# A two-layer decoder step on one core: order of the dense block's product and weight split, clearing of the query tables, the router's token rows, and where the expert gates are computed

## The chip, the cores and the metric

One NeuronCore of a Trainium2 chip runs one launch of a hand-ordered kernel: every engine (TensorE as PE, ScalarE as ACT, VectorE as DVE, GpSimd as POOL, SyncE as SP) has its own instruction list, and semaphores tie the lists together. The metric is the device time of the launch in microseconds (us), median of several runs.

## The reference, cut to what matters

288 tokens (256 of a prompt, 32 of eight sample requests) of width 1024 go through two layers, in float32.

```python
# each layer
x = x + rmsnorm_concat(mixer_a, mixer_b, mixer_x)(rmsnorm(x) @ w_in) @ w_out
# layer 0: dense SwiGLU, D_FF = 2816
x = x + (silu(h @ wg) * (h @ wu)) @ wd          # h = rmsnorm(x) * g_ffn[0]
# layer 1: 8 experts, D_FF_E = 3584, each token uses its 2 best
logits = h @ w_router                           # h = rmsnorm(x) * g_ffn[1]
vals, idx = top_k(logits, 2)
gates = one_hot(idx) weighted by softmax(vals)
x = x + sum_e gates[:, e] * swiglu(h, wg[e], wu[e], wd[e])
y = rmsnorm(x) * g_final
```

Further outputs are memory keys and values, pooling buffers and v rows of the mixers.

## The kernel before, in words

**Weight stream.** All weights come as 402 chunks of 128x2048 floats (1 MB). SP loads chunk c into one of six `raw` slots as soon as chunk c-6 is split (`load_chunk`, line 299). ACT copies it to `whi` as fp32r (line 306) once chunk c-3 has been used by PE, and DVE writes the remainder into `wlo` (line 310). Products use three matmuls each, hi x hi, hi x lo, lo x hi (`mm3`, lines 322 to 324). PE counts used chunks in `chunk_used`. `hi_static` and `lo_static` put these splits at fixed places in the lists of ACT and DVE, so the order of everything is written out by hand.

**Start.** PE turns the memory rows, computes keys and values of both layers (lines 1430 to 1450), turns x, spreads the row norms over all partitions (`spread_rstd`, line 1410; DVE scales the identity into `diag`, line 879, and keeps the product as `rB`, line 886), and begins layer 0.

**A layer's first part.** `queries(k)` for eight blocks, then four transposes of the keys (line 1476), which DVE copies as `kT` (line 925); DVE scales the queries into `qT` (line 921) and spreads the sample queries into the tables `qs_hi` and `qs_lo` (lines 937, 940), which POOL clears first (`zero_pair`, line 439). Scores are line 1490. In layer 1 POOL adds up the squares of x (`power_of_x`), PE sums them (`sums_of_x`, after `queries(5)`), DVE makes the mean, POOL the power -0.5, DVE `diag`, PE spreads it; POOL clears the two tables and a block of `xn` right after the power.

**A layer's end of mixing.** After `sample_values(1)` PE waits for ACT's `os_rows` (line 648), folds the samples (line 1617), then alternates three transposes (line 1391) with the output projection of one block (`turn`, `project_left`). ACT writes the turned block's hi part, DVE its lo part (line 850); DVE's list has `scale_rows` of three groups and the splits of chunks c0+13 and c0+14 in between.

**Dense block.** `up(f)` multiplies one gate and one up column block per chunk, 22 chunks, 48 matmuls each; it waits for `gp_out` of two chunks before. DVE's `hidden(f)`: two products with `rB` (lines 1055, 1056), then the split of chunk f+3, then, after ACT's silu (line 685), three products into `HT_hi`, `us`, `HT_lo` (lines 1059 to 1062). ACT's list is silu(f), then the hi part of chunk f+3. `down(i, j)` (PE) starts by waiting for `x_dense`; DVE raises it by two after all 22 `hidden` (line 1069).

**Router and start of the experts.** PE forms the logits (`route`), turns xT into token rows x (line 1717) and the logits into rows (line 1724). ACT copies the rows (line 707). DVE makes top two, mask, and with line 1098 the normalised rows `xm` of tiles 0 and 2 (POOL tile 1, lines 495, 496) with the gains that SP loads over a constant (line 387). ACT takes the exponentials (line 712), DVE the gates (lines 1132 to 1144), positions, target rows, number of rounds (line 1170) and the selection `sel` of expert 0 (line 1188). In the round loop ACT and DVE first split three chunks, PE gathers the tokens of expert 0 (line 1753), ACT and DVE split the gathered block (lines 737, 1244), and `gate_up` begins. ACT evaluates silu for the experts in line 742.

## Time and profile before

| | us |
|---|---|
| three runs | 1537.89, 1538.41, 1539.53 |
| median | 1538.41 |
| the profiled execution | 1538.45 |
| its span, first to last instruction | 1536.7 |
| granted TensorE clock, mean | 0.98 of full speed |
| PE, DVE, ACT, POOL busy | 1460.1, 1181.8, 950.5, 116.8 |
| HBM read | 434.63 MB, mean 297 GB/s over the span |

The busy times overlap. The profile's time of an instruction is its start and its own duration, a bracket behind it is the idle time of its engine just before it and who ended it. Matmuls are pipelined: the distance between starts tells their rate, not their durations.

### The profile page before, as it was taken

To read this page: it belongs to the slowest core of one execution; us is meant where nothing else is said; L and a number is where in the kernel's file an instruction comes from. 1 tells how busy PE (TensorE), PEld (TensorE's weight loads), DVE (VectorE), ACT (ScalarE), POOL (GpSimd) and SP (SyncE) were. 2 spreads that over 40 slices of the span, in tenths; PEclk is the share of its full clock that TensorE was granted. 3 is DMA by queue.
4 is the path that set the end of the run, shared out by engine and by line. 5 is a ranking of instruction groups with operands and counts; after the bars stand their busy time and mean duration, and the time that the engine had idled before them with its cause. 6 is when DMAs were issued, how large, how long until landed. Compare 5 with 4: busy or idle time off the path is not lost.

```text
span 1536.7 us, 21608 instructions
## 1 busy us (share of the span) xinstructions
PE 1460.1 (95%) x7664; PEld 1239.0 (81%) x7664; DVE 1181.8 (77%) x1111; ACT 950.5 (62%) x908; POOL 116.8 (8%) x134
## 2 busy tenths in 40 slices
PE   6899999969898799999999999999999999999996
PEld 5788999969788678888888888888888887888774
DVE  6536566644636678898888898888889889889996
ACT  6535333334335467777777777777777777777773
POOL 1211211000310310000000000000000000001011
PEclk8999999989899899999999999999999999999998
DMA  9523566635433199999999999999999999999991
GB/s 371 195 110 138 206 251 248 241 135 181 149 115 133 69 350 370 369 372 369 367 363 392 373 354 394 370 354 386 365 365 393 372 365 361 373 362 364 388 386 71
DMA packets 67426, 456.85 MB, mean 297 GB/s; under 512 B 7652, under 2 KB 7946, under 8 KB 15783
## 3 DMA queue, kind: packets, MB, share of 16 engines
q1 hardware_dynamic: 59687, 428.43, 73.3%
q0 software_dynamic: 5680, 20.49, 3.4%
q10 hardware_dynamic: 2016, 7.34, 1.2%
q8 instruction: 28, 0.46, 0.1%
q14 instruction: 15, 0.12, 0.0%
HBM read 434.63 MB, written 21.88 MB: 297 GB/s over the span
## 4 chain that ended last, share of the span: by engine, by line
PE 81%; DVE 8%; ACT 5%; issue 5%; POOL 0%; DVEq 0%; DMA 0%; ACTq 0%; POOLq 0%; SPq 0%
PE bank L322 25%; PE bank L324 25%; PE bank L323 25%; ACT whi L306 4%; PE bank L1782 2%; DVE wlo L310 2%; DVE HT_hi L1059 1%; DVE gs L1056 1%; PE bank L1753 1%; DVE us L1060 1%; DVE us L1055 1%; DVE x L1239 0%; ACT junk L543 0%; PE bank L1553 0%; PE bank L1760 0%
## 5 line engine op out<-in xcount | busy, mean ns | idle before, releaser
L310 DVE TENSOR_TENSOR wlo<-raw,whi 128x2048 fp32r<-128x2048 f32 x402 | 920.9, 2292 | 243.8 <-ACT whi L306 242.7
L306 ACT ACTIVATE whi<-raw 128x2048 fp32r<-128x2048 f32 x402 | 769.1, 1915 | 161.8 <-PE bank L324 160.9
L322 PE MATMUL bank<-whi,gT_hi 128*128 128x512 f32 x896 | 363.4, 406 | 1.5 <-DVE gT_lo L1244 1.5
L324 PE MATMUL bank<-whi,gT_lo 128*128 128x512 f32 x896 | 354.4, 396 | 0.0
L323 PE MATMUL bank<-wlo,gT_hi 128*128 128x512 f32 x896 | 352.8, 394 | 0.0
L324 PEld LDWEIGHTS bank<-whi,gT_lo 128*128 128x128 f32 x896 | 168.4, 188 | 39.4
L322 PEld LDWEIGHTS bank<-whi,gT_hi 128*128 128x128 f32 x896 | 169.2, 189 | 35.6 <-issue 1.7
L323 PEld LDWEIGHTS bank<-wlo,gT_hi 128*128 128x128 f32 x896 | 169.2, 189 | 34.6
L322 PE MATMUL bank<-whi,eT_hi 128*128 128x512 f32 x448 | 177.3, 396 | 1.0 <-DVE eT_lo L1259 1.0
L323 PE MATMUL bank<-wlo,eT_hi 128*128 128x512 f32 x448 | 177.0, 395 | 0.0
L324 PE MATMUL bank<-whi,eT_lo 128*128 128x512 f32 x448 | 176.1, 393 | 0.0
L322 PE MATMUL bank<-hT_hi,whi 128*128 128x288 f32 x512 | 155.1, 303 | 10.6 <-DVE hT_lo L850 4.9
L323 PE MATMUL bank<-hT_lo,whi 128*128 128x288 f32 x512 | 151.6, 296 | 0.0
L324 PE MATMUL bank<-hT_hi,wlo 128*128 128x288 f32 x512 | 151.6, 296 | 0.0
L746 ACT ACTIVATE eT_hi<-bank 128x256 fp32r<-128x256 f32 x112 | 43.3, 386 | 124.7 <-PE bank L1782 124.7
L322 PEld LDWEIGHTS bank<-hT_hi,whi 128*128 128x128 f32 x512 | 96.7, 189 | 17.3 <-DVE gs L1056 7.0
L322 PEld LDWEIGHTS bank<-whi,eT_hi 128*128 128x128 f32 x448 | 84.2, 188 | 21.2 <-issue 1.4
L324 PEld LDWEIGHTS bank<-whi,eT_lo 128*128 128x128 f32 x448 | 84.5, 189 | 20.0
L323 PEld LDWEIGHTS bank<-wlo,eT_hi 128*128 128x128 f32 x448 | 84.5, 189 | 19.4
L323 PEld LDWEIGHTS bank<-hT_lo,whi 128*128 128x128 f32 x512 | 96.7, 189 | 0.0
L324 PEld LDWEIGHTS bank<-hT_hi,wlo 128*128 128x128 f32 x512 | 96.7, 189 | 0.0
L520 POOL TENSOR_TENSOR tick<-half 128x3 f32<-128x3 f32 x2 | 3.0, 1512 | 912.9 <-DMA y_slots<-y_rows 865.8
(248 smaller groups left out, 1474.6 us busy)
## 6 DMA issues: line engine op xcount, KB each, us to landing
raw<-in_stream SPq DMA_DIRECT2D x402, 1024.0 KB, 5.8
x_slots<-zero POOLq DMA_DIRECT2D x18, 640.0 KB, 4.3
rows_e<-x_slots ACTq DMA_DIRECT2D x7, 512.0 KB, 5.3
y_slots<-y_rows ACTq DMA_DIRECT2D x7, 512.0 KB, 6.3
const<-in_const SPq DMA_DIRECT2D x1, 1192.0 KB, 21.8
stage<-in_mem SPq DMA_DIRECT2D x2, 512.0 KB, 4.2
xn<-in_x_prompt SPq DMA_DIRECT2D x1, 1024.0 KB, 11.4
out_y_prompt<-xm SPq DMA_DIRECT2D x2, 512.0 KB, 2.6
```

Source lines behind the costliest of these rows:

```text
L306: nc.scalar.activation(whi[:, slot % SPL, :], raw[:, slot, :], ACT.Copy).then_inc(hi_ready, 1)
L310: nc.vector.tensor_tensor(wlo[:, slot % SPL, :], raw[:, slot, :], whi[:, slot % SPL, :].bitcast(F), ALU.subtract).then_inc(lo_ready, 1)
L322: nc.tensor.matmul(out, a_hi, b_hi, start=start, stop=False, **kw)
L323: nc.tensor.matmul(out, a_hi, b_lo, start=False, stop=False, **kw)
L324: return nc.tensor.matmul(out, a_lo, b_hi, start=False, stop=stop, **kw)
L746: nc.scalar.activation(eT_hi[:, s % 2, :, :].rearrange("p a b -> p (a b)"), bank[4 + s % 2][:, 0:256], ACT.Copy).then_inc(S["eT_hi_out"], 1)
L1055: V.tensor_tensor(us[:, j % 2, :], bank[b + 1][:, 0:NT], rB[:, :], ALU.mult)
L1056: V.tensor_tensor(gs[:, j % 2, :], bank[b][:, 0:NT], rB[:, :], ALU.mult).then_inc(S["gp_out"], 1)
L1059: V.tensor_tensor(rows(HT_hi), gs[:, j % 2, :], us[:, j % 2, :], ALU.mult)
L1060: V.tensor_tensor(us[:, j % 2, :], gs[:, j % 2, :], us[:, j % 2, :], ALU.mult).then_inc(S["hf_out"], 1)
L1753: last = T.matmul(bank[b][:, (k % 4) * P:(k % 4 + 1) * P], xm[:, t, k * P:(k + 1) * P], sel[:, t, :], start=t == 0, stop=t == 2)
L1782: last = T.transpose(bank[4 + s % 2][:, b * P:(b + 1) * P], eh[:, s % 2, b * P:(b + 1) * P], ident)
```

## The change: what it does

1. **Start.** ACT executes one tiny Copy before it waits for its first data. The norms are spread inside the transposes of x (after block 4), not after them; DVE splits chunk 5 after the loop.
2. **First part.** Key transposes and the copy `kT` stand before the queries. In layer 1 the squares are summed after `queries(3)`. The two query tables are allocated where the first eight blocks of HT lie; HT is one tile with hi and lo side by side. POOL clears the tables in the down stage, before the last addition of squares, once all but the last chunk is used; the block of `xn` is cleared after the masks.
3. **End of mixing.** ACT squares two tiles of `ob` and splits c0+13 earlier, evicts `os_rows` after two turned blocks; PE folds the samples inside the projection's first block. DVE's lo parts of blocks 0, 1 and 2 move ahead of a scaling and of the split of c0+13.
4. **Dense block.** In `hidden` the three products stand before the split of chunk f+3. `x_dense` is raised before all `hidden`. The spread of the norms lies inside `up(1)`.
5. **Router.** xm is not made from x any more: PE multiplies hT_hi and hT_lo (gains are in them) by an fp32r identity and ACT evicts with the norm as scale, six times. The turning of x follows after the position matmuls. `g_moe` is no longer loaded. The first two expert chunks are split in layer 1's dense-norm stage; in round 0 one split is left (an inner hardware loop from `(1 >> r) * 2` to 3). Exponentials and gates are computed inside the round, after the gathered block's split. `select(0)` comes ahead of the target rows, and again at a round's end.

```diff
             act.wait_ge(preset, 1)
+            link(nc.scalar.activation(junk[:, 0:3], half[:, :], ACT.Copy))
             act.wait_ge(first_in, 16)
...
             def power_of_x(u, n):
                 for k in range(KD):
+                    if u == 1 and k == KD - 1:
+                        pool.wait_ge(chunk_used, C_DOWN + DOWN_CH - 1)
+                        zero_pair(qs)
                     pool.wait_ge(sq_out, KD * u + k + 1)
...
                 if l:
                     power_of_x(1, N_MIX)
-                    zero_pair(qs)
-                    nc.gpsimd.memset(xn[:, 2, :], 0.0).then_inc(S["xn_blank"], 1)
                     pool.dma_start(table[:, :], io["table"][1]).then_inc(table_in[1], 16)
...
# ACT, end of mixing
                 hi_static(act, c0 + 11, c0 + 12)
+                act.wait_ge(S["op_out"], l + 1)
+                sum_squares(ob, N_O, (0, 1), signal=False)
                 act.wait_ge(S["a_out"], l + 1)
                 sum_squares(ug, N_A)
+                hi_static(act, c0 + 13)
                 act.wait_ge(S["b_out"], l + 1)
                 sum_squares(b_rows, N_B)
+                turn_hi(l, (0, 1))
                 act.wait_ge(chunk_used, c0 + 12)
                 nc.scalar.activation(os_rows[:, :], bank[6][:, 0:DX], ACT.Copy, scale=rden[:, 8:9])\
                     .then_inc(S["os_rows_out"], 1)
-                turn_hi(l, (0, 1))
-                hi_static(act, c0 + 13)
                 act.wait_ge(S["os_done"], l + 1)
...
-                sum_squares(ob, N_O)
+                sum_squares(ob, N_O, (2,))
...
-                if l == 0:
-                    hi_static(act, C_UP)
+                c_next = (C_UP, C_MOE)[l]
+                hi_static(act, c_next)
...
# DVE, end of mixing
                 scale_rows(ug, rstd_event(l, E_A), N_A, cols=slice(0, DA))
+                turn_lo(l, (0, 1))
                 scale_rows(b_rows, rstd_event(l, E_B), N_B, cols=slice(DA, DA + DB))
-                turn_lo(l, (0, 1))
+                turn_lo(l, (2,))
                 lo_static(dve, c0 + 13)
-                turn_lo(l, (2,))
                 scale_rows(ob, rstd_event(l, E_O), N_O, cols=slice(DA + DB, D))
...
# DVE, hidden(f)
                         V.tensor_tensor(gs[:, j % 2, :], bank[b][:, 0:NT], rB[:, :], ALU.mult).then_inc(S["gp_out"], 1)
-                        split()
                         dve.wait_ge(S["silu_out"], f + 1)
...
                             .then_inc(S["H_out"], 1)
+                        split()
+                    dve.sem_inc(S["x_dense"], 2)
                     with V.Fori(0, NF // RAWS) as i:
...
-                    dve.sem_inc(S["x_dense"], 2)
                     for m in range(KD // 2):
...
# ACT, router
+            for t in range(3):
+                if t == 2:
+                    act.wait_ge(S["xm_blank"], 1)
+                for n in range(2):
+                    act.wait_ge(S["xm_turned"], 2 * t + n + 1)
+                    nc.scalar.activation(xm[0:ROWS[t], t, n * 512:(n + 1) * 512], bank[ROW_BANKS[2 * t + n]][0:ROWS[t], :],
+                                         ACT.Copy, scale=rstd[0:ROWS[t], N_FFN, t:t + 1]).then_inc(S["xm_out"], 1)
...
# ACT, round
-                for off in (-2, -1, 0):
-                    hi(cb, lap, off)
+                with nc.scalar.Fori(nc.scalar.snap((1 >> r) * 2), 3) as m:
+                    act.wait_ge(chunk_used, cb + (m - 2) - SPL + 1)
+                    at = bass.ds(nc.scalar.snap(m * CW), CW)
+                    nc.scalar.activation(flat(whi)[:, at], flat(raw)[:, at], ACT.Copy).then_inc(hi_ready, 1)
                 for b in range(2):
                     gathered_hi(q, 0, b)
+                act.wait_ge(S["logit_out"], 1)
+                for t in range(3):
+                    rr = ROWS[t]
+                    last = nc.scalar.activation(expo[0:rr, t, :], logits[0:rr, t, :], ACT.Exp, bias=nfirst[0:rr, t:t + 1],
+                                                scale=rstd[0:rr, N_FFN, t:t + 1])
+                last.then_inc(S["exp2_out"], 1)
                 hi(cb, lap, 1)
...
# PE, layer start
+                pe.wait_ge(S["kv_out"], l + 1)
...
                 last.then_inc(S["kT_done"], 1)
+                for k in range(KD):
+                    queries(k)
+                    if l and k == 3:
+                        sums_of_x(1, 0)
...
# PE, end of mixing and dense block
+                    if k == 0:
+                        fold_samples()
...
-                    up(1, 1)
-                    spread_rstd(2, 1)
+                    up(1, 1, lambda: spread_rstd(2, 1))
...
# PE, router
+            def gained_rows(t):
+                for n in range(2):
+                    for k in range(4 * n, 4 * n + 4):
+                        out = bank[ROW_BANKS[2 * t + n]][0:ROWS[t], (k % 4) * P:(k % 4 + 1) * P]
+                        tok = slice(t * P, t * P + ROWS[t])
+                        T.matmul(out, hT_hi[:, k, tok], ident_r[:, :], start=True, stop=False)
+                        last = T.matmul(out, hT_lo[:, k, tok], ident_r[:, :], start=False, stop=True)
+                    last.then_inc(S["xm_turned"], 1)
```

## Rows read from the trace of the kernel before

**Rows 1.** Waits of PE, in total, times, longest.
```profile
PE bank L1410 <- DVE diag L879: 4.3, 1, 4.3
```
**Rows 2.** Windows of the down and expert stages: busy (instructions) by engine, clock, DMA share, GB/s.
```profile
340.00:360.00 20.00, 20.00 (x152) 20.00 (x151) 9.71 (x9) 8.94 (x10) 2.16 (x3) 1.00 0.57 195
...
600.00:640.00 40.00, 40.00 (x179) 32.42 (x178) 35.44 (x24) 29.16 (x25) 0.00 (x0) 1.00 0.96 367
```
**Rows 3.** Timeline at the start: start, duration, engine, line, [idle before].
```profile
8.25 1.28 ACT L559 ACT_TABLE_LOAD   x1 [8.25 <-DVE xT L890]
...
15.43 0.80 PE L322 MATMUL bank<-whi,hT_hi 128*128 128x512 f32 x1 [7.03 <-DVE wlo L310]
```
**Rows 4.** Timeline, queries and scores of layer 0.
```profile
46.72 0.40 PE L322 MATMUL bank<-hT_hi,whi 128*128 128x288 f32 x1 [2.83 <-DVE rB L886]
...
54.14 0.68 DVE L925 COPY kT<-bank 128x512 f32<-128x512 f32 x1
...
56.34 1.14 PE L1490 MATMUL bank<-kT,qT 64*128 64x256 f32 x8 [0.24 <-DVE qs_lo L940]
```
**Rows 5.** Timeline, end of mixing in layer 0.
```profile
125.62 0.63 PE L1617 MATMUL bank<-os_rows,const 128*32 128x64 f32 x8 [1.47 <-ACT os_rows L648]
```
**Rows 6.** Timeline, third chunk of the dense block.
```profile
174.60 0.40 PE L322 MATMUL bank<-hT_hi,whi 128*128 128x288 f32 x1 [1.67 <-DVE gs L1056]
```
**Rows 7.** Timeline, one turn of the dense loop on PE, ACT and DVE.
```profile
288.25 0.40 PE L322 MATMUL bank<-hT_hi,whi 128*128 128x288 f32 x1
...
295.00 0.37 PE L322 MATMUL bank<-hT_hi,whi 128*128 128x288 f32 x1
...
288.58 1.90 ACT L306 ACTIVATE whi<-raw 128x2048 fp32r<-128x2048 f32 x1
...
290.51 2.29 DVE L310 TENSOR_TENSOR wlo<-raw,whi 128x2048 fp32r<-128x2048 f32 x1 [2.32 <-ACT whi L306]
...
294.04 0.45 DVE L1055 TENSOR_TENSOR us<-bank,rB 128x288 f32<-128x288 f32 x1
```
**Rows 8.** Timeline, start of the down stage on PE.
```profile
320.11 0.60 PE L322 MATMUL bank<-HT_hi,whi 128*128 128x288 f32 x1 [11.92 <-DVEq L1069]
...
325.31 0.35 PE L322 MATMUL bank<-HT_hi,whi 128*128 128x288 f32 x1
```
**Rows 9.** Timeline, norms spread: once in layer 0, the rest in layer 1.
```profile
31.64 0.63 DVE L879 TENSOR_SCALAR diag<-const,rstd 128x128 f32<-128x128 f32 x3
...
399.65 2.01 POOL L439 MEMSET qs_hi<- 128x2304 f32 x1
...
399.71 5.08 DVE L879 TENSOR_SCALAR diag<-const,rstd 128x128 f32<-128x128 f32 x3 [1.05 <-POOL rstd L435]
...
408.35 3.78 PE L1490 MATMUL bank<-kT,qT 64*128 64x256 f32 x16 [2.17 <-DVE kT L925]
```
**Rows 10.** Timeline, router and start of the experts.
```profile
518.21 1.03 PE L1717 MATMUL bank<-const,xT 128*128 128x128 f32 x8
...
524.51 3.44 DVE L1098 SCALAR_TENSOR_TENSOR xm<-x,rstd,const 128x1024 f32<-128x1024 f32 x1
...
531.50 0.15 DVE L1170 TENSOR_TENSOR rounds<-over 1x1 int32<-1x1 f32 x1
...
534.03 5.51 ACT L306 ACTIVATE whi<-raw 128x2048 fp32r<-128x2048 f32 x3
...
534.24 8.57 PE L1753 MATMUL bank<-sel,xm 128*128 128x128 f32 x48 [8.21 <-DVE sel L1188]
...
542.85 0.60 ACT L737 ACTIVATE gT_hi<-bank 128x512 fp32r<-128x512 f32 x1 [2.49 <-PE bank L1753]
...
544.30 0.49 PE L322 MATMUL bank<-whi,gT_hi 128*128 128x512 f32 x1 [1.49 <-DVE gT_lo L1244]
```
**Rows 11.** Table loads of ACT: in the dense loop, and all of line 742.
```profile
210.25 1.28 ACT L685 ACT_TABLE_LOAD   x1
...
L742 ACT ACT_TABLE_LOAD  x1: 1283/1283/1283, 549.3 to 549.3; - x1
```

More of the change, by code:

```diff
@@ L65 @@
 FILL_LEFT = NE * SLOTS - FILL * (UP_CH - UP_CH % RAWS)
-SETTLES = 7
+SETTLES = 11
 NEVER = -3.0e38
@@ L708, in _ @@
                                          ACT.Copy).then_inc(S["x_rows_out"], 1)
-            for t in range(3):
-                r = ROWS[t]
-                act.wait_ge(S["logit_out"], 1)
-                last = nc.scalar.activation(expo[0:r, t, :], logits[0:r, t, :], ACT.Exp, bias=nfirst[0:r, t:t + 1],
-                                            scale=rstd[0:r, N_FFN, t:t + 1])
-            last.then_inc(S["exp2_out"], 1)
             act.wait_ge(S["rounds_ok"], 1)
@@ L1153, in _, with select @@
                 r = ROWS[t]
-                last = V.tensor_tensor(posm[0:r, t, :], posm[0:r, t, :], bank[2][0:r, P_AT + t * NE:P_AT + (t + 1) * NE], ALU.add)
+                last = V.tensor_tensor(posm[0:r, t, :], posm[0:r, t, :], bank[1][0:r, P_AT + t * NE:P_AT + (t + 1) * NE], ALU.add)
             link(last)
+            link(V.reduce_max(cmax[:, :], bank[1][0:1, P_AT + 3 * NE:P_AT + 4 * NE], AX.X))
+            V.tensor_scalar(over[:, 0:1], cmax[:, :], float(P), 1.0, ALU.is_gt, ALU.add)
+            link(V.tensor_scalar(over[:, 1:2], cmax[:, :], float(2 * P), None, ALU.is_gt))
+            V.tensor_tensor(rounds[:, :], over[:, 0:1], over[:, 1:2], ALU.add).then_inc(S["rounds_ok"], 1)
+            def select(e):
+                for t in range(3):
+                    last = V.tensor_scalar(sel[:, t, :], slots[:, :], posm[:, t, e:e + 1], None, ALU.is_equal)
+                last.then_inc(S["sel_out"], 1)
+            select(0)
             for t in range(3):
@@ L1183, in lo @@
                     split_lo(dve, cb + off + RAWS * extra, (off + 2) % RAWS)
-                def select(e):
-                    for t in range(3):
-                        last = V.tensor_scalar(sel[:, t, :], slots[:, :], posm[:, t, e:e + 1], None, ALU.is_equal)
-                    last.then_inc(S["sel_out"], 1)
                 n_settled = [0]
@@ L1365, in _ @@
                 dve.wait_ge(S["pos_moved"], r + 1)
-            dve.wait_ge(gain_in, 32)
+                select(0)
+            dve.wait_ge(gain_in, 16)
             for t in range(3):
@@ L1467, in queries @@
                         m.then_inc(chunk_used, 1)
-                for k in range(KD):
-                    queries(k)
-                    if l and k == 5:
-                        sums_of_x(1, 0)
-                pe.wait_ge(S["kv_out"], DEPTH)
+                pe.wait_ge(S["kv_out"], l + 1)
                 for f in range(2):
@@ L1613, in _, with fold_samples @@
                 sample_values(1)
-                pe.wait_ge(S["os_rows_out"], l + 1)
-                for h in range(HEADS):
-                    last = T.matmul(bank[7][0:NS, h * HD:(h + 1) * HD], fold[:, h, :], os_rows[:, h * HD:(h + 1) * HD],
-                                    start=True, stop=True)
-                last.then_inc(S["os_done"], 1)
+                def fold_samples():
+                    pe.wait_ge(S["os_rows_out"], l + 1)
+                    for h in range(HEADS):
+                        last = T.matmul(bank[7][0:NS, h * HD:(h + 1) * HD], fold[:, h, :], os_rows[:, h * HD:(h + 1) * HD],
+                                        start=True, stop=True)
+                    last.then_inc(S["os_done"], 1)
                 def project(k, *ds):
@@ L1681, in up @@
                         for k in range(KD):
+                            if middle and k == 5:
+                                middle()
                             for w in range(2):
```

196 lines of the change are left out of this document (92 added, 104 removed).

## The prediction

> **What bounds the kernel now.** I read the windows first, then PE's waits, then the timelines of each stretch in which PE is idle. From about 545 us to the end the experts run, and there PE is busy 40.00 of 40 us, at full clock, with DVE at 35.44 and ACT at 29.16 and DMA at 0.96 [rows 2]. Nothing in the change shortens a product there, so some 975 us are to stay as they are. What can move lies before: PE's own idle stretches (the brackets [rows 1, 3 to 8, 10]), matmuls at the lower clock level right behind a long one, and the dense loop, whose pitch is longer than its 48 matmuls. The order of reading matters: the page's 95% for PE hides that the idle part stands almost whole on the chain to the end, since PE is its busiest engine in every stage.
>
> In the down stage 152 matmuls of 288 columns start in 20 us, 0.1316 us each, at full clock (2.4 GHz) [rows 2]: this is the full rate used below.
>
> **The parts and their sum.**
>
> (1) *First Copy early.* ACT's table load of 1.28 us starts only at 8.25, when the first data are there; the first weight split and PE's first product at 15.43 follow behind it [rows 3]. Moved under the first DMAs it is free. Bounds: 0 (if a chunk's arrival is the next limit) and 1.28; the 7.03 us of idle are DVE's and ACT's chain, so I take 1.3.
>
> (2) *Start of layer 0.* PE is idle for 2.83 us before the queries, for `rB` [rows 4]. With the spread four blocks earlier and DVE's 2.29 us split [rows 7] behind the loop, this idle goes. Behind the queries, the copy `kT` (0.68 us) no longer stands between `qT` and the sample tables, on which the scores at 56.34 waited [rows 4]. The four key transposes are moved, not saved. 2.83 + 0.68 = 3.5; the end of the x transposes may now hold the last query, so 2.8 to 3.9, taken 3.4.
>
> (3) *Fold.* The idle of 1.47 us for `os_rows` [rows 5] goes, in each layer. But what is late next is DVE: turned block 2, then the split of c0+13 (2.29 us [rows 7]), a scaling, then block 3, while PE has one block and three transposes, 12 x 0.1316 + 3 x 0.13 = 2.0 us [rows 2, 10]. Most of the gain is given back there. Bounds 0 and 2 x 1.47 = 2.9; taken 1.0 for both layers, nearer to the nil end.
>
> (4) *Spread inside `up(1)`.* PE waited 1.67 us for the first `gs` [rows 6]; the diagonal has to be ready five eighths into the chunk. 0.8 to 1.7, taken 1.6.
>
> (5) *Dense loop.* From 174.60 to 288.25 there are 17 turns, 6.685 us each, and single ones reach 6.75 [rows 6, 7]. PE needs 48 x 0.1316 = 6.32 [rows 2]. The pitch is that of a ring: two products of DVE, silu, ACT's split 1.90, DVE's split 2.29, three products, and only then the next `gs`, for which PE waits: 5 x 0.45 less overlaps + 0.45 + 1.90 + 2.29 = 6.7 [rows 7]. In the new order the three products (1.35) run beside ACT's split, and the ring is 0.9 + 0.45 + 1.90 + 2.29 = 5.5, under PE's 6.32. So PE sets the pitch. I take 6.41, a little for the loop's edges: 20 x (6.685 - 6.41) = 5.5. Bounds: 3.0 if half is lost at the edges, 7.3 at the bare rate.
>
> (6) *Down stage.* PE stands still for 11.92 us before its first down product, for DVE's count that is raised only behind all 22 tiles [rows 8]. Then 21 matmuls take 325.31 - 320.11 = 5.20 us at the lower level (1.2 GHz), 2.76 at the full rate: 2.4 lost. With `x_dense` raised early, PE waits only for the tile that it needs. The last is finished about 0.9 + 0.45 + 1.35 = 2.7 us after the last `up` [rows 7], and PE reaches it after 21 x 3 x 0.1316 = 8.3 us. The two first chunks are split in time too (the split of the second one ends before the last `up` does). Gain 11.9 + 2.4 = 14.3; 12 to 14.4, taken 14.2. This is the largest term.
>
> (7) *Start of layer 1.* Idle 4.26 us for the diagonal and 2.17 for `kT` [rows 1, 9]. The three scalings of the diagonal took 5.08 us while POOL cleared tables, 0.63 where POOL did not [rows 9]. The clearing (2 x 2.01) goes under the last down products, whose 42 x 0.1316 = 5.5 us cover it, before an addition that waits for ACT anyway. If that cover failed, the 4 us would stand before the last addition. PE's remaining idle is the copy of `rB` and two scalings, about 1.5 us, and 0.5 for the sample tables: 6.43 - 2.0 = 4.4. The 16 scores took 3.78 us, at full clock 2 x 1.14 = 2.28 [rows 4, 9]; that 1.5, the spread itself and the first sample products, at the lower level too, give 2.9 more if the clock stays up, as it did behind the 2.83 us idle of layer 0 [rows 4]. 7.3 in all; 5 to 8.5.
>
> (8) *Router to first expert product.* Now from 518.2 to 544.30 [rows 10]. The new path on PE: sums 0.6; 48 gained-row matmuls of 128 columns, which the trace does not have: by columns 128/288 x 0.1316 = 0.058, as transposes 1.03/8 = 0.13 [rows 2, 10]; I take 0.11, nearest the transposes (same shape), 5.3; logit transposes and position matmuls about 1.8. Positions at 525.9. DVE's 3.44 us for tile 0 [rows 10] and the gates are gone from its queue, and `rounds` and `sel` need about 1.8: 527.7 (now 531.65 for `rounds` [rows 10]). PE turns xT, 24 x 0.13 = 3.1: 529.0; loop entry about 1; the gather, 8.57 now and mostly at the lower level [rows 10], between 4.3 and 8.6, taken 5.2: 535.2. ACT has six evictions more in its queue, 12 x 0.6 by the 0.60 of a gathered block [rows 10], and is free at 530; table load 1.28 and one split, 5.51/3 = 1.84, not three: 534. DVE's one split, 2.29, ends at 536.3, two gathered blocks behind it at 537.7. First product at 538.0, gain 6.3. Behind it, exponentials and gates (some 2.5 us) lie before the split of the chunk that PE needs three chunks later, 3 x 12 matmuls or some 8 us; without that cover they would cost their 2.5. PE is idle 2.8 us before its first product and may start at the lower level, up to 2.5 lost. The two splits moved into the norm stage of layer 1 may push the last lo parts into `route` by 0.4. Taken 5.9; 3 to 8.5. `g_moe`'s DMA is gone from SP's queue ahead of six loads that wait for slots anyway: nothing.
>
> (9) *Tail.* `select(0)` once more, three small operations (about 0.7) beside ACT's squares: 0 to 0.3 lost, taken 0.1.
>
> Sum: 1.3 + 3.4 + 1.0 + 1.6 + 5.5 + 14.2 + 7.3 + 5.9 - 0.1 = 40.1. The profiled execution took 1538.45, 0.04 over the median, so the forecast is 1538.4 - 40.1 = **1498.3 us**. The lower ends add to 26 (1512), the upper ones to 48 (1490).
>
> **A rule against part (8).** The table load shows 1.28 us, and the ones in the dense loop were in ACT's idle time before a wait [rows 11]. The Trainium skill, page "ScalarE: Activation LUTs", section "What ACT_TABLE_LOAD costs", gives 2.66 us for every switch of set, the load and a drain, and its section on table sets wants one set's calls done together; the change puts an exponential between copies and silu. By that price and one more switch on the path, the forecast would be 1501; the trace has no drain behind a load (load and next start are one load apart), so the sum goes by the row.
>
> **Rivals.**
>
> *A: the middle is refilled.* DVE or ACT has in the dense loop and at the router less slack than I drew: (5) stays at half and (8) at 1, as ACT, with six more evictions and a loop inside a loop, becomes the last one there. For it: ACT is the engine with the most new work before the first product. Against: two splits, 3.7 us, leave the same queue. 1498.3 + 2.7 + 4.9 = 1506.
>
> *B: the early down start is only half one.* If down(0) waits for tiles or weight chunks one by one, the 11.92 shrinks to, say, half, and the lower clock level stays: 6 + 2.4 lost, 1506.7. Against: the tile arithmetic in (6), 2.7 against 8.3 us.
>
> *C: slower than before.* Exp now lies within the round's loop. Should a table load be placed before each of the experts' 112 silus, each 1.28 us, of which about 0.6 falls in ACT's idle time and 0.7 delays the hidden tile, this costs 112 x 0.7 = 78 us: 1576. It decides from 40.1/112 = 0.36 us per step on. For it: the dense loop does load once per pass [rows 11]. Against: of line 742 there is one load now, though exp stands just before that loop too [rows 11].
>
> *D: the change doesn't do what it says at the dense loop*: PE's 6.685 is a cost of the loop itself, not of DVE. Then (5) is 0: 1503.8. Against: the gap at a turn's edge varies with `gs`.
>
> **Chances.** Forecast (within 4 us) 0.60, A 0.15, B 0.05, C 0.03, D 0.07, better than the forecast by over 4 us (gathers and gained rows at their low ends) 0.10. A measurement of this kernel tells a change of 0.2%, 3 us, from none. All but C are faster: 0.96, same 0.01, slower 0.03. The range reaches to A, B and D, and below to 1491: 1491 to 1508.
>
> **What would show it.** Down starts within 0.5 us of the last `up`, with no lower clock there; the dense pitch is 6.3 to 6.45; the diagonal in layer 1 takes under 1 us; the wait for `sel` before the gather is gone or under 2 us; one wait for `hT_lo` of about 1.5 us stands at the fourth block of mixing's end; first expert product at about 504 (544.3 - 40.2); ACT table loads of line 742 stay one. I am wrong if the experts' stage, 544.30 to the end, is over 3 us longer than now, or if PE's idle before down is over 3 us.

## The result and the profile after

The changed kernel took 1502.34 us (median of four runs, 1499.53 to 1504.76) against 1538.15 (1537.72 to 1539.53): 0.9765 of the time, 95% interval [0.9743, 0.9787], 35.8 us less. The forecast was 1498.3 with a range of 1491 to 1508. The profiled execution took 1504.31 us, its span 1502.6. One execution of rows_pool (1599.4 us, mean granted clock 0.85) and one of the kernel before (1824.8 us, 0.75) were disturbed and are left out of all figures.

PE's waits in the whole of the changed kernel (what it waited for, us in total, times, longest):

```profile
PE bank L321 <- DVE hT_lo L859: 8.2, 6, 1.6
PE bank L321 <- DVE wlo L309: 5.5, 1, 5.5
PE bank L1427 <- DMA stage<-in_mem: 5.3, 1, 5.3
PE bank L1800 <- DVE eh L1235: 3.8, 8, 2.0
PE bank L321 <- DVE gT_lo L1225: 3.3, 1, 3.3
```

The wait for the diagonal [rows 1] is gone, and so are 11.92 us before down [rows 8] and 8.21 before the gather [rows 10]. (`wlo` 5.5 is the start, where PE waited 7.03 [rows 3].) The first line, the waits for the turned blocks at mixing's end, is three waits in each layer, 1.2 to 1.6 us each; the prediction's last part had one of about 1.5. They are not new: the kernel before had five of them beside its two waits for `os_rows` (1.47 and 1.52):

```profile
PE bank L322 <- DVE hT_lo L850: 4.9, 5, 1.3
```

Timelines of the changed kernel (start, us, engine, line, what it writes and reads; the bracket is the idle time before and what ended it). First the down stage and the start of layer 1:

```profile
295.05 0.29 PE L321 MATMUL bank<-HT,whi 128*128 128x288 f32 x1
295.18 0.30 PE L322 MATMUL bank<-HT,whi 128*128 128x288 f32 x1
...
369.88 0.64 DVE L888 TENSOR_SCALAR diag<-const,rstd 128x128 f32<-128x128 f32 x3 [1.05 <-POOL rstd L436]
...
373.93 1.14 PE L1490 MATMUL bank<-kT,qT 64*128 64x256 f32 x8 [1.53 <-issue]
```

Down starts without a wait, at full clock (0.13 us from matmul to matmul), the diagonal takes 0.64 us instead of 5.08, and the scores stand at 373.93, 34.4 us earlier than 408.35 [rows 9]. Then the router:

```profile
485.61 0.27 PE L1728 MATMUL bank<-ident_r,hT_hi 128*128 128x128 f32 x1
485.72 0.35 PE L1729 MATMUL bank<-ident_r,hT_lo 128*128 128x128 f32 x1
485.87 0.42 PE L1728 MATMUL bank<-ident_r,hT_hi 128*128 128x128 f32 x1
486.09 0.41 PE L1729 MATMUL bank<-ident_r,hT_lo 128*128 128x128 f32 x1
...
491.85 4.85 PE L1755 MATMUL bank<-const,xT 128*128 128x128 f32 x24
496.54 5.52 PE L1771 MATMUL bank<-sel,xm 128*128 128x128 f32 x48
505.36 0.50 PE L321 MATMUL bank<-whi,gT_hi 128*128 128x512 f32 x1 [3.30 <-DVE gT_lo L1225]
```

In the middle of the gained rows the step from one matmul to the next doubles from 0.11 to 0.21 us: the granted clock falls from full to half (1.2 GHz) while PE is busy without a gap, and stays there until 496.0; the 48 matmuls of the gather behind it run at full rate.

How the gain stands at milestones, by the step of the prediction (us, the profiled executions):

| Up to | before | after | gain | of which step | forecast |
|---|---|---|---|---|---|
| first product | 15.43 | 14.40 | 1.0 | (1) 1.0 | 1.3 |
| layer 0, second scores | 56.34 | 51.27 | 5.1 | (2) 4.0 | 3.4 |
| first `up` | 158.79 | 153.33 | 5.5 | (3), layer 0: 0.4 | 1.0 with layer 1 |
| last down product | 392.82 | 364.15 | 28.7 | (4) to (6) 23.2 | 21.3 |
| router starts | 514.03 | 477.82 | 36.2 | (7), (3) of layer 1: 7.5 | 7.3 + rest of (3) |
| first expert product | 544.30 | 505.36 | 38.9 | (8) 2.7 | 5.9 |
| end | 1536.7 | 1502.6 | 34.1 | experts' stage and tail, -4.8 | -0.1 |

Two things are off by more than 2 us: the router gave 2.7 in place of 5.9, and the experts' stage, which was to stay as it was, grew by 4.7 us.

### The profile page after: what moved, and what is told of

It is laid out like the page before. It is cut to its first block, busy times and chain, and to the rows that moved or that the text cites. A ratio compares the mean times of both kernels' runs of the same rounds, so it can differ in the third digit from the quotient of the medians.

```text
span 1502.6 us, 21721 instructions
## 1 busy us (share of the span) xinstructions
PE 1455.8 (97%) x7712; PEld 1239.2 (82%) x7712; DVE 1175.2 (78%) x1113; ACT 952.2 (63%) x914; POOL 112.2 (7%) x132
## 4 chain that ended last, share of the span: by engine, by line
PE 89%; ACT 3%; DVE 3%; issue 2%; ACTq 0%; POOL 0%; DMA 0%; DVEq 0%; POOLq 0%; SPq 0%
PE bank L321 28%; PE bank L323 28%; PE bank L322 28%; ACT whi L305 2%; PE bank L1800 2%; DVE wlo L309 1%; ACT junk L537 1%; DVE x L1220 1%; PE bank L1553 0%; PE bank L1778 0%; DVE stage L1008 0%; PE bank L1755 0%; ACTq L776 0%; DMA stage<-in_mem 0%; DVE hT_lo L859 0%
## 5 line engine op out<-in xcount | busy, mean ns | idle before, releaser
L321 PEld LDWEIGHTS bank<-hT_hi,whi 128*128 128x128 f32 x512 | 96.4, 188 | 10.2 <-DVE hT_lo L859 9.6
## 6 DMA issues: line engine op xcount, KB each, us to landing
const<-in_const SPq DMA_DIRECT2D x1, 1192.0 KB, 21.7
```

The costliest lines, as they stand in the source:

```text
L321: nc.tensor.matmul(out, a_hi, b_hi, start=start, stop=False, **kw)
```

## Experiments

"Stretch R" is the time from the last router matmul to the first expert product (before: 518.08 to 544.30, 26.22 us), "stage E" that from there to the end of the span (before 992.4; tail included). The scores of layer 1 stand at 373.3 to 375.5 in the nine profiles whose kernel is the changed one up to there, so a difference of 1 or 2 us in that column is scatter. Runs of one group ran on the same chip, beside the kernel before (1537.6, 1539.4, 1538.1, 1538.7 us).

| Kernel | us, median (all) | ratio to before, 95% | layer-1 scores | R | E |
|---|---|---|---|---|---|
| changed | 1502.34 (1499.5-1504.8) | 0.9765 [0.9743, 0.9787] | 373.93 | 23.12 | 997.2 |
| u_split | 1512.45 (1511.7-1512.8) | 0.9830 [0.9813, 0.9847] | 387.10 | 18.55 | 996.8 |
| u_count | 1507.08 (1506.6-1507.4) | 0.9795 [0.9778, 0.9812] | 380.38 | 18.55 | 995.5 |
| u_start1 | 1508.16 (1505.1-1509.5) | 0.9806 [0.9789, 0.9823] | 377.81 | 18.55 | 996.9 |
| warm | 1498.02 (1497.3-1498.9) | 0.9739 [0.9723, 0.9756] | 373.30 | 18.55 | 993.9 |
| after2 (changed, again) | 1504.43 (1501.1-1504.7) | 0.9768 [0.9754, 0.9782] | 374.53 | 23.12 | 997.0 |
| u_both | 1521.05 (1520.1-1521.6) | 0.9885 [0.9869, 0.9901] | 395.61 | 18.54 | 996.8 |
| u_pre | 1504.46 (1504.0-1504.8) | 0.9777 [0.9762, 0.9793] | 374.10 | 24.80 | 994.3 |
| rows_pool | 1501.59 (1498.5-1501.6) | 0.9759 [0.9741, 0.9778] | 375.45 | 18.56 | 994.5 |
| u_gates | 1504.49 (1500.0-1505.1) | 0.9773 [0.9755, 0.9790] | 375.05 | 24.99 | 994.9 |
| swap | 1498.72 (1496.0-1499.4) | 0.9740 [0.9725, 0.9755] | 375.32 | 18.31 | 995.4 |
| swap_pool | 1495.91 (1494.4-1496.2) | 0.9723 [0.9709, 0.9736] | 374.55 | 16.75 | 993.4 |
| wide | 1502.71 (1501.7-1503.4) | 0.9766 [0.9752, 0.9779] | 373.42 | 21.60 | 996.6 |

**The dense loop and the count: u_split, u_count, u_both**

```diff
 # u_split, in hidden(), DVE
+                        split()
                         dve.wait_ge(S["silu_out"], f + 1)
...
-                        split()
```

> The changed kernel with DVE's weight split put back between its first two products and the wait for silu, in the dense loop; nothing else. Theory (ring of the dense loop): the ring grows from 5.5 to 6.7 us, over PE's 6.32, so the pitch goes from about 6.4 back to 6.6 to 6.7 and the kernel is slower than the changed one by 4 to 6 us. Rival (the 6.685 us of before were a cost of the loop itself, and the layout of HT or the edges took it away): the pitch stays at 6.4, and the time within 1 us. Were the down stage's first tile late through it, PE would wait there before its first down product, some 1 to 2 us on top.

```diff
 # u_count, DVE, around the 22 tiles
-                    dve.sem_inc(S["x_dense"], 2)
...
                         hidden(f, f, lambda: lo_static(dve, C_UP + 3 + f))
+                    dve.sem_inc(S["x_dense"], 2)
```

> The changed kernel with DVE's count x_dense raised behind all hidden tiles again; nothing else. Theory: PE stands still before its first down product for the last tile's silu, products and splits, about 10 to 12 us, then runs some 20 matmuls at the lower clock (2.4 us): slower than the changed kernel by 12 to 14.3 us. Rival (with the split behind the products the last tiles are done sooner, so that the count is no longer what PE waited for in this size): idle of 3 to 6 us, slower by 4 to 8.

u_both makes both edits.

> The changed kernel with both of two parts undone: DVE's weight split again ahead of the wait for silu, and the count x_dense again behind all hidden tiles. Each alone made it slower, by 10 us (the split) and by 5 us (the count). Theory: the wait before the first down product is mostly due to late tiles and shared by both, so that together they bring back the 11.9 us of before: slower than the changed kernel by 19 to 23 us, more than the sum of the two, 15. Rival: they add up, 14 to 16.

PE's first down product in u_split, u_count and u_both:

```profile
313.32 0.61 PE L321 MATMUL bank<-HT,whi 128*128 128x288 f32 x1 [3.94 <-DVE HT L1070]
```

```profile
299.29 0.39 PE L321 MATMUL bank<-HT,whi 128*128 128x288 f32 x1 [3.34 <-DVEq L1077]
```

```profile
314.47 0.60 PE L321 MATMUL bank<-HT,whi 128*128 128x288 f32 x1 [11.93 <-DVEq L1077]
```

(In u_split this is the first product that waited; its down stage had begun at 300.88.) From one product of `gs` to the next it is 6.37 us in the changed kernel, 6.37 in u_count and 6.69 in u_split: the order of DVE's queue sets the pitch, and the ring theory holds to 0.04 us of its figure (6.41). But the late tiles cost more than the pitch: at the scores of layer 1 u_split is 13.2 us behind the changed kernel, 5.8 of it from the loop, 3.9 from the wait and about 2.8 from matmuls at 1.2 GHz behind it (313.3 to 319). My 4 to 6 us, with 1 to 2 for a late tile, were too small. The count alone gives 6.5 us there (the wait is 3.3, not 10 to 12: the rival of that run was right), both together 21.7. So the 11.92 us [rows 8] were one wait with two causes. What shows it is the waits: 3.9 and 3.3 us with one cause, 11.93 with both. In the position of the scores the pair is only 2 us over the sum of the two, 13.2 + 6.5 = 19.7, which is no more than the scatter there; in the times, over the 1500.6 us that the changed kernel takes when its clock does not fall at the router (see after2), it is 11.8, 6.5 and 20.4.

**Clearing at layer 1's start: u_start1**

```diff
-                    if u == 1 and k == KD - 1:
-                        pool.wait_ge(chunk_used, C_DOWN + DOWN_CH - 1)
-                        zero_pair(qs)
...
                     power_of_x(1, N_MIX)
+                    zero_pair(qs)
+                    nc.gpsimd.memset(xn[:, 2, :], 0.0).then_inc(S["xn_blank"], 1)
...
-                if l:
-                    nc.gpsimd.memset(xn[:, 2, :], 0.0).then_inc(S["xn_blank"], 1)
```

> The changed kernel with the query tables and xn's rows cleared by POOL at the start of layer 1 again, behind the norm sum; nothing else. Theory: the diagonal's scalings stand beside POOL's clearing and take some 5 us in place of under 1; PE is idle for 4 us more and starts at the lower clock: slower than the changed kernel by 4 to 8 us. Rival (the scalings were slow for another reason, or the spread and the sample tables now end last): within 1.5 us.

DVE's diagonal and PE's wait for it in u_start1:

```profile
370.39 5.08 DVE L885 TENSOR_SCALAR diag<-const,rstd 128x128 f32<-128x128 f32 x3 [1.05 <-POOL rstd L433]
```

```profile
375.53 0.75 PE L1408 MATMUL bank<-diag,const 128*128 128x288 f32 x2 [3.10 <-DVE diag L885]
```

The three scalings take 5.08 us again, to the hundredth [rows 9]. The scores come 3.9 us later and mixing's end in layer 1 5.7 later (453.44 against 447.78). Of both, 0.5 us lies ahead of the edit (last down product at 364.66 against 364.15), so the clearing costs 3.4 and 5.2 us; the 1.8 between them falls behind the wait, where the granted clock was at 1.2 GHz from 376.8 to 383.6. The median, 1508.16, is 5.8 us over the changed kernel's, within the 4 to 8 expected. So the same three DVE instructions take eight times as long with POOL at work beside them.

**The router's clock: after2, warm, wide**

after2 is the changed kernel once more, with no edit.

> The changed kernel itself, once more. In its first four runs it took 1499.5, 1500.4, 1504.3 and 1504.8 us; the profiled one was the third of these by size and had TensorE at 1.2 GHz from 485.8 to 497.5 us, in the middle of the router's matmuls. The kernel with added matmuls behind the gather has the same code up to there and had no such fall. Theory (the fall is no property of the code but comes in some executions): the times lie in two groups, near 1500 and near 1504.5, and an execution of the upper group has the fall, one of the lower does not; the stretch from the last router matmul to the first expert product is 23.1 us with the fall and some 18.6 to 19 without. Rival (the fall always comes at this code): every profile has it.

```diff
 # warm, PE, behind the gather
                 gather(1)
                 pe.wait_ge(S["x_rows_out"], 6)
+                for _ in range(12):
+                    T.matmul(bank[6][:, :], ident_r[:, :], whi[:, 0, 0:512], start=True, stop=True)
+                pe.wait_ge(S["x_rows_out"], 6)
```

> The changed kernel with 12 matmuls of 512 columns, whose result nobody reads, put on PE between the gather and the first expert product, where it was idle for 3.3 us and afterwards ran the first 3.6 us at 1.2 GHz; it adds work. Theory (that idle time brought the lower clock): the first expert products run at full clock, and the kernel is faster than the changed one by 1 to 1.6 us, or by as much less as the added matmuls reach past the idle time. Rival (the lower clock there is the tail of the fall at 485.8 us, or has nothing to do with the idle time): the lower clock stays, and the time is the same or 0.5 us longer.

The nine executions of the changed kernel lie in two groups, 1499.5 to 1501.5 (four) and 1504.3 to 1504.8 (five). The mean granted clock of an execution is 0.989 to 0.991 in the upper group and 0.993 to 0.994 in the lower. Both profiles are of the upper group, both have the fall (485.8 and 486.2 us, for 10.2 us each), and both have R = 23.12; of the lower group, mean 1500.6, there is no profile. Six kernels with the same router code and no fall there in their profile have 18.54 to 18.56. The fall costs 4.57 us in R, and by the times it comes in some executions and not in others; a program that differs from the changed kernel only behind the gather, warm, shows none. Its windows from 484 us on (us, busy time by engine, PEclk, DMA), and those of the changed kernel:

```profile
484.00:486.00 2.00, 2.00 (x20) 1.90 (x19) 0.14 (x1) 0.78 (x2) 0.85 (x1) 1.00 0.00 0
486.00:488.00 2.00, 2.00 (x22) 2.00 (x21) 1.61 (x19) 1.20 (x3) 0.00 (x0) 1.00 0.00 0
```

```profile
484.00:486.00 2.00, 2.00 (x19) 1.90 (x19) 0.67 (x9) 1.29 (x2) 0.29 (x1) 0.94 0.00 0
486.00:488.00 2.00, 2.00 (x11) 2.00 (x11) 1.78 (x13) 0.69 (x1) 0.00 (x0) 0.50 0.00 0
```

The lower clock behind the first expert product has another cause. In warm it is gone together with the 3.3 us of idle time that the twelve matmuls fill (PE waits 0.52 us), while it is there in every profile that keeps the wait of 3.3 us. E falls from 997.2 to 993.9, of which 1.6 is this and 1.6 a second low stretch, 3.4 us long from 1264.0 in the changed kernel, that warm does not have either. That one stands behind a wait of 1.96 us for `eh`, which all fourteen profiles have; seven of them show the low clock behind it and seven don't. The time, 1498.02, is 2.6 us under the lower group.

```diff
 # wide, PE, in gained_rows()
                         last = T.matmul(out, hT_lo[:, k, tok], ident_r[:, :], start=False, stop=True)
+                        if k % 2:
+                            T.matmul(bank[0][:, :], ident_r[:, :], sPT[0][:, 0:512], start=True, stop=True)
```

> The changed kernel with 24 matmuls of 512 columns, whose result nobody reads, put between the gained-row matmuls of 128 columns at the router (one behind every fourth of them); it adds work, 24 x 0.23 = 5.5 us on PE, of which little is hidden. In the changed kernel the clock fell to 1.2 GHz in the middle of these small matmuls in about half of the executions (485.8 us in both profiles taken), while PE was busy without a gap for more than 3 us. Theory (PE's stream of small matmuls lets the clock fall, and wide ones among them keep it up): no execution has the fall; all five times lie within 1.5 us of each other, near 1500.5 + 5 = 1505.5 to 1506.5. Rival (the fall doesn't depend on the kind of the matmuls there): in about half of the executions it comes as before, and the times fall in two groups 4 us apart, near 1506 and 1510.

The number of matmuls there is wrong: one behind every fourth of 48 is 12, and 12 x 0.23 = 2.8 us. By that the theory gives 1500.6 (mean of the lower group) + 2.8 = 1503.4, the rival 1503.4 and 1507.4. All five executions took 1501.7 to 1503.4 and the profile has no fall:

```profile
486.00:488.00 2.00, 2.00 (x18) 1.87 (x16) 1.70 (x16) 0.69 (x1) 0.00 (x0) 1.00 0.00 0
488.00:490.00 2.00, 2.00 (x20) 1.51 (x20) 0.54 (x4) 1.27 (x2) 0.00 (x0) 1.00 0.00 0
```

So with more work in the router the kernel is never in the slower group. Were the chance of a fall 5 in 9 as in the changed kernel, five without would come 1 time in 60. It does not show that the shape of the matmuls decides: six kernels with the router's matmuls untouched (u_split, u_count, u_both, u_pre, warm, swap_pool) had no second group either, in 25 executions, and no fall there in their profiles. So the chance of a fall differs between kernels for another reason, which no run here names; u_gates has it in three of four by the times, and rows_pool's times, 1498.5 and twice 1501.6, look like two groups too. The Trainium skill, page "TensorE: Matmul & The Clock Gate", section "HAM oscillation — how this bites in real kernels", ties such falls to PE waiting for data between groups of matmuls; that agrees with the low stretches behind the waits at 313.32 and 505.36, and not with this one, where the trace has no wait.

**The two splits moved into layer 1's norm stage: u_pre**

```diff
-                c_next = (C_UP, C_MOE)[l]
-                hi_static(act, c_next)
+                if l == 0:
+                    hi_static(act, C_UP)
...
-                with nc.scalar.Fori(nc.scalar.snap((1 >> r) * 2), 3) as m:
+                with nc.scalar.Fori(0, 3) as m:
```

(and the same for the second chunk and for DVE's halves)

> The changed kernel with the two weight chunks of the first expert split by ACT and DVE at the router again, three in a row, and not in the norm stage of layer 1. Theory: two splits more on ACT ahead of the gathered blocks, 2 x 1.84 = 3.7 us, and DVE's behind them: the first expert product comes 3.5 to 5 us later, and the norm stage ends up to 0.4 us sooner: slower by 3 to 4.6 us. Rival (ACT and DVE have idle time for them while PE turns rows, and the gather ends last): within 1 us.

ACT in u_pre, and PE's first expert product:

```profile
494.97 1.28 ACT L814 ACT_TABLE_LOAD   x1 [0.64 <-issue]
496.26 1.91 ACT L814 ACTIVATE whi<-raw  x1
498.19 1.28 ACT L814 ACT_TABLE_LOAD   x1
499.48 1.91 ACT L814 ACTIVATE whi<-raw  x1
501.41 1.28 ACT L814 ACT_TABLE_LOAD   x1
502.70 1.91 ACT L814 ACTIVATE whi<-raw  x1
```

```profile
508.41 0.79 PE L321 MATMUL bank<-whi,gT_hi 128*128 128x512 f32 x1 [9.54 <-DVE gT_lo L1228]
```

R is 24.80, 6.2 us over the 18.55 without a fall; I had expected 3.5 to 5. Each pass of this loop loads ACT's table again, although nothing but copies runs in it, so a chunk costs 1.28 + 1.91 = 3.2 us there and not 1.84 as in the straight code of before [rows 10]. Of the 6.2 us the time shows 3.9 (over the lower group of the changed kernel, 1500.6): E is 2.9 us shorter than there, ACT's DMA issue being a short one and no lower clock coming at 1264 us.

**Gates ahead of the loop: u_gates**

```diff
 # ACT
                                          ACT.Copy).then_inc(S["x_rows_out"], 1)
+            act.wait_ge(S["logit_out"], 1)
+            for t in range(3):
+                rr = ROWS[t]
+                last = nc.scalar.activation(expo[0:rr, t, :], logits[0:rr, t, :], ACT.Exp, bias=nfirst[0:rr, t:t + 1],
+                                            scale=rstd[0:rr, N_FFN, t:t + 1])
+            last.then_inc(S["exp2_out"], 1)
             act.wait_ge(S["rounds_ok"], 1)
 # DVE, behind the counts
+            dve.wait_ge(S["exp2_out"], 1)
+            for t in range(3):
+                rr = ROWS[t]
+                last = V.tensor_tensor(gate[0:rr, t, :], expo[0:rr, t, :], mask[0:rr, t, :], ALU.mult)
...
```

(and the same lines taken out of the round)

> The changed kernel with the exponentials (ACT) and the gates (DVE) put back ahead of the round's loop: ACT's three behind its six evictions of x, DVE's twelve behind the counts. Theory: they lie on ACT's queue between the evictions and the weight split that ends before the first expert product; the exponentials and one more table load delay it by 0.94 + 1.28 = 2.2 us; DVE's 1.4 us are hidden beside ACT's split: slower than the changed kernel by 2 to 2.5 us, the stretch from the last router matmul to the first expert product 20.6 to 21.1 us in place of 18.6. Rival (the table load is made anyway at the loop, so only 0.9 us come on top, or nothing, PE's gather ending last): 0 to 1 us.

The profile has the fall of the clock, R is 24.99, 1.87 over the changed kernel's 23.12 with the fall, and PE's wait for `gT_lo` 5.2 in place of 3.3. That is near the theory's 2.2. Yet the times are those of the changed kernel, 1500.0 without and 1504.3 to 1505.1 with the fall: E is 994.9, 2.3 us shorter, since ACT's slow DMA issue (next) was 1.19 us here and hidden, and the low stretch at 1264 was absent. A step on the path at one place was paid back at another.

**ACT's slow issue: rows_pool**

```diff
-                        act.wait_ge(x_spread, 16 * 6)
-                        nc.scalar.dma_start(rows_e[:, :], x_slots[slot_rows(e + 1), :]).then_inc(rows_in, 16)
 # POOL
+                pool.wait_ge(x_spread, 16 * 6)
+                for e in range(NE - 1):
+                    pool.wait_ge(S["gat_hi"], r * (2 * NE) + (2 * e + 2))
+                    pool.dma_start(rows_e[:, :], x_slots[bass.ds(nc.gpsimd.snap(r * P + (e + 1) * SLOTS), P), :])\
+                        .then_inc(rows_in, 16)
```

> The changed kernel with the DMA that loads the next expert's rows issued by POOL, as soon as the gathered rows of the one before are out, in place of ACT. At the first expert ACT's issue took 3.7 us in all profiles of the changed kernel (0.41 before), with ACT idle for 3.0 and PE late by some 1.1 to 1.5 us behind it. In the same interval a small transfer of a queue that carries instructions falls each time. Theory (ACT waits there for its own next instructions, and the issue only shows it): ACT has an idle stretch of some 3 us at about the same place without any issue, and the time is the same within 0.5 us. Rival (the issue itself is slow, since it meets the busy queues): the stretch is gone, and the kernel is faster by 1 to 1.5 us.

The issue in the changed kernel with what ACT did next, the same stretch of rows_pool, and the issues of u_pre and u_gates:

```profile
527.93 3.84 ACTq L776 DMA_DIRECT2D rows_e<-x_slots  x1
532.07 0.38 ACT L741 ACTIVATE esg<-bank 128x256 f32<-128x256 f32 x1 [2.97 <-issue]
```

```profile
525.31 1.92 ACT L305 ACTIVATE whi<-raw 128x2048 fp32r<-128x2048 f32 x1 [0.59 <-PE bank L323]
527.14 0.36 ACT L745 ACTIVATE esg<-bank 128x256 f32<-128x256 f32 x1
528.10 1.92 ACT L305 ACTIVATE whi<-raw 128x2048 fp32r<-128x2048 f32 x1 [0.60 <-PE bank L323]
```

```profile
530.92 0.41 ACTq L777 DMA_DIRECT2D rows_e<-x_slots  x1
```

```profile
531.80 1.19 ACTq L780 DMA_DIRECT2D rows_e<-x_slots  x1
```

ACT's idle stretch is gone with the issue: the rival of that run holds. The profiled execution, 1498.47 us, is 2.1 under the lower group. E is 994.5, and its DVE steps come at the distances of before, where the changed kernel lost 1.4 us in the first expert. What makes the issue slow stays open. In the nine profiles in which it took 3.4 to 3.84 us a small transfer of one of the queues that carry instructions (8 KB) began 1.9 to 2.3 us behind its start, in u_gates (1.19 us) 0.4 ahead of it, and in all ten the issue ended 1.56 to 1.58 us behind the start of that transfer. In u_pre and in the kernel before, the issue of 0.41 us was over 2.1 and 8.4 us before the transfer began. So the issue's end goes with the transfer to 0.02 us, as it would if ACT waited for its own next instructions; but no run moved the transfer by itself, and why the issue stands until then is not shown.

**Gathered rows first: swap, swap_pool**

```diff
 # ACT and DVE, ahead of the first expert
+                for b in range(2):
+                    gathered_hi(q, 0, b)
                 for slot in range(3):
                     act.wait_ge(raw_full[slot], 16 * lap + 16)
                 with nc.scalar.Fori(nc.scalar.snap((1 >> r) * 2), 3) as m:
...
-                for b in range(2):
-                    gathered_hi(q, 0, b)
```

> The changed kernel with the two steps ahead of the first expert exchanged on ACT and on DVE: first the gathered rows are turned to hi and lo, then the third weight chunk is split. PE needs that chunk only two chunks (24 matmuls, 5.5 us) behind its first expert product, while the gathered rows gate the first product itself. Theory (in the changed kernel the first product waits 3.3 us for gT_lo only because DVE's 2.29 us split, and ACT's table load and split before it, stand ahead of it in the queues): the wait shrinks to about 1.3 us or less, the first product comes 2 to 2.7 us earlier, and the kernel is faster by 1.5 to 2.7 us if the third chunk is there in time (in all 1498 to 1499 without the fall of the clock at the router, 1502 with it). Rival (the third chunk then comes later than PE needs it and the wait only moves there): first product earlier, a new wait of 1 to 2.5 us two chunks behind it, the time within 0.7 us.

swap_pool adds rows_pool's edit.

> The changed kernel with both the exchange ahead of the first expert and the next expert's rows loaded by POOL in place of ACT. Theory (the two gains lie at different places and add): 2 us from the exchange and some 2 us from the removed 3.7 us issue (the experts' stage took 994.5 us with it gone, 997.2 in the changed kernel with another lower-clock stretch of 1.6 us in it): about 1496.5 to 1498 in executions without the fall of the clock at the router, 1500.5 to 1502 with it. Rival: PE is bound by other waits in the first expert, and the sum is under 2 us: 1498.5 to 1500 without the fall.

DVE and PE in swap:

```profile
501.10 0.69 DVE L1225 TENSOR_TENSOR gT_lo<-bank,gT_hi 128x512 fp32r<-128x512 f32 x1 [1.99 <-ACT gT_hi L736]
503.32 2.29 DVE L1336 TENSOR_TENSOR wlo<-raw,whi  x1 [1.53 <-ACT whi L815]
505.53 0.30 DVE L1341 TENSOR_TENSOR gate<-expo,mask 128x8 f32<-128x8 f32 x3
```

```profile
501.92 0.50 PE L321 MATMUL bank<-whi,gT_hi 128*128 128x512 f32 x1 [1.49 <-DVE gT_lo L1225]
```

The third chunk's lo part is ready at 505.6 and PE needs it 5.5 us behind 501.92, at 507.4: no new wait. PE's wait shrinks from 3.3 to 1.49 us, R to 16.75 without a fall (swap's own profile has a short one, 18.31), and the clock stays up behind the first product. swap_pool took 1495.91 us, 8.4 less than the changed kernel's median of nine (1504.31), 4.7 less than its lower group (1500.6). All five times are under the 1496.5 to 1498 that the theory gave, so the two gains add at least in full; swap alone is 1.9 under the lower group by its median. It is the fastest of all kernels here, 0.9723 of before.

## Why the prediction was right, and where it was not

**(1), (2)** held within 0.6 us. **(3)**: layer 0 gave 0.4, but not by the term that I had. The stretch from the products of line 1600, ahead of mixing's end, to the first `up`, before and after (us, PE, PEld, DVE, ACT, POOL, PEclk, DMA):

```profile
112.76:158.79 46.03, 42.14 (x320) 40.70 (x321) 31.70 (x51) 26.48 (x45) 8.26 (x10) 0.96 0.43 155
107.70:153.33 45.63, 41.21 (x320) 39.41 (x321) 31.27 (x51) 26.38 (x45) 8.15 (x10) 1.00 0.44 156
```

PE's idle time grew from 3.9 to 4.4 us: the wait for `os_rows` went, and three waits for turned blocks (1.60, 1.20, 1.30) stand where two stood (0.82, 1.30). The gain is PE's shorter busy time, which goes with the granted clock: before ran at 1.2 GHz from 127.4 to 130.8 us, the changed kernel did not.

**(4) to (6)**, 23.2 for 21.3. The pitch came out at 6.37, the down stage without a wait. What the runs corrected is the account, not the sum: I gave 14.2 us to the count. Undone alone it costs 6.5, and the loop's order, for which I had 5.5, costs 13.2, since it also brings the last tiles in time. Rival B is out since down starts without any wait, rival D since the pitch goes from 6.37 to 6.69 with DVE's order alone.

**(7)** 7.5 with layer 1's share of (3), for 7.3; by u_start1 the clearing is 5.2 of it, 3.4 at the scores, most of it idle, and 1.8 behind them at the lower clock. The mechanism was right.

**(8)** is where the step failed in the profiled execution: 2.7 for 5.9. Term by term, without a fall of the clock R is 18.55, a gain of 26.22 - 18.55 = 7.7 for the 6.3 of the path, so the tiles and queues were drawn well, even a little low (I had PE's gather and ACT's evictions late). What I did not price is that the clock could fall while PE is busy: I looked for lower clock only behind idle time, and called the gained rows 0.11 us each throughout. In five of nine executions, by their times, it fell among them and took 4.57 us. Rival A named ACT as the last one there, and so it is, as in my own working: in warm, without a fall,

```profile
490.83 2.99 ACT L710 ACTIVATE x<-bank 128x512 f32<-128x512 f32 x6 [0.78 <-PE bank L1755]
494.64 1.28 ACT L813 ACT_TABLE_LOAD   x1 [0.82 <-issue]
498.02 2.29 DVE L1334 TENSOR_TENSOR wlo<-raw,whi  x1 [5.03 <-ACT whi L813]
492.81 5.53 PE L1771 MATMUL bank<-sel,xm 128*128 128x128 f32 x48
```

PE's gather ends at 498.3, and DVE's split, which waited 5.03 us for ACT's, stands ahead of the gathered rows. What did not come is A's price, a gain of 1 in (8). With the fall the evictions are paced by PE's turns at half rate. That ACT's and DVE's split stood in front of the gathered rows was in my working as given; swap shows it to be worth 1.8 us and free to change.

**The experts' stage** was to keep its 992.4 us, and I had written that over 3 us more would prove me wrong. It grew by 4.7 (with the tail 4.8), so by that sign this part was wrong. By the runs this is 1.6 of lower clock behind the first product (gone in warm), 1.6 at 1264 us behind a wait of 1.96 us for `eh` that before had as well without a fall, and 1.4 from ACT's issue (gone in rows_pool). I had named the first, up to 2.5 us, but in (8)'s range and not in the sum.

**(9)** -0.1 for -0.1. **Rival C** is out: ACT loads a table once at line 741, and DVE, which takes what line 741 writes, is busy with a split until 514.2.

```profile
511.94 1.28 ACT L741 ACT_TABLE_LOAD   x1
513.24 0.38 ACT L741 ACTIVATE esg<-bank 128x256 f32<-128x256 f32 x1
```

The mechanism it feared, a load per pass of a loop, is real in the loop of the first splits, as u_pre shows; there it costs one load of 1.28 us on the path. The price by the Trainium skill (page "ScalarE: Activation LUTs", section "What ACT_TABLE_LOAD costs", 2.66 us) does not show here either: at 511.94, between the exponentials and the experts' first silu, there is one load of 1.28, and the silu follows at once.

In the profiled execution 34.1 us stand against 40.1: 4.6 less by the fall and 4.8 by the experts' stage and tail, and some 3 more by (2), (4) to (6) and (8)'s path than forecast. By the medians, with the fall in half of the executions, it is 35.8. Part of the agreement is thus a cancelling of errors. And by the time alone, 4.0 us over the forecast, rival D (1503.8) was nearer than the forecast; it is the pitch that rules it out. Of the signs listed, the down stage's start, the pitch, the diagonal, the wait for `sel` and the table loads came as said; the one wait at mixing's end and the length of the experts' stage did not.

## What to carry to other kernels

A wait in front of a stage can have two causes in series, a late counter and late data; undo each by itself and both together before saying what one is worth, since here waits of 3.3 and 3.9 us with one cause made 11.9 with both. Where PE stands still before the first product of a stage, ask of each step in front of it on the other engines' queues whether that product needs it, or one five microseconds later: putting the gathered rows ahead of the third chunk's split was free. And where the times of one program lie in two groups, compare profiles within a group: the fall of 4.6 us at the router was larger than most edits tried here.

## What the chip showed that was not expected

The granted clock fell from 2.4 to 1.2 GHz in the middle of an unbroken run of 128-column matmuls (0.11 us apart, at 485.8 us), in some executions of one program and not in others; with a 512-column matmul behind every fourth, in none of five, but in six other kernels without such matmuls in none of 25 either. Behind one and the same wait of 1.96 us it fell in seven of fourteen profiles. The ACT table is loaded in every pass of a loop that holds only copies (1.28 us each). A DMA issue on ACT took 3.4 to 3.8 us in place of 0.41 at the first of seven places in ten of twelve profiles (1.19 in one of these), and held up ACT's next activation by 3 us in the changed kernel; it ended 1.56 to 1.58 us behind the start of a transfer of an instruction queue in all ten, and with the issue moved to POOL, ACT ran on. Three scalings on DVE took 5.08 us beside POOL's clearing and 0.64 without.
